# Token routing and the first expert blocks in one program, with the token numbers of two blocks computed on chip

## The reference

```python
h2 = rms_norm(x, norm_ffn_g)
y  = hierarchical_moe(h2, ...)
x  = x + y

def hierarchical_moe(h, ...):
    g_logits = h @ w_rg + b_rg                 # 4 groups
    grp      = argmax(g_logits)
    e_in     = (h @ w_re + b_re)[grp]          # 8 experts of that group
    top_p, top_e = top_k(softmax(e_in), 2)
    gate   = p_grp * top_p / sum(top_p)
    expert = grp * 8 + top_e                   # 2 of 32 experts for each token
    # assignments sorted by expert, each expert padded to blocks of 128 slots
    pos = pstart[expert] + rank_within_expert
    slot_tok[pos] = token
    for block:                                 # 128 slots, one expert
        gu = h[slot_tok] @ w_up[e];  g, u = split(gu)
        yb = (silu(g) * u) @ w_down[e]
    y[token] += gate * yb[pos]
```

## Time and profile before

| | |
|---|---|
| median of 3 runs | 1874.7 us (1873.71 to 1875.47) |
| profiled execution, its own time | 1877.97 us |
| its span | 1876.4 us |
| first instructions of `route` | 1201.1 us from the span's start |
| first transpose of `experts` on TensorE | 1265.2 us |
| transpose of block 2's tokens | 1291.9 us |
| busy share of the span | PE 91%, DVE 70%, ACT 44%, POOL 22% |

### The profile page before, as it was taken

The page is one execution under the profiler, slowest core; times in us unless marked ns, Lnnn a source line. Parts: engine busy times, 40 slices in busy tenths (PEclk is TensorE's granted clock), DMA queues, the critical chain, the costliest instruction groups (busy, mean ns, idle before and its releaser), DMA issues. The chain is left out here.

```text
span 1876.4 us, 25514 instructions
## 1 busy us (share of the span) xinstructions
PE 1704.8 (91%) x8546; PEld 1413.3 (75%) x8546; DVE 1322.0 (70%) x1800; ACT 823.3 (44%) x968; POOL 414.1 (22%) x311
## 2 busy tenths in 40 slices
PE   6999989999999988999969888509999999999995
PEld 5877778887888867899858677407888888887774
DVE  4257894899990028777449832446999999989895
ACT  5355321211121134567521211306777777767673
POOL 1211320232222210000012000052333232334342
PEclk8999999999999989999969899859999999999998
DMA  4722341332222546457076332429999999999992
GB/s 157 202 101 101 140 147 52 116 113 90 92 90 105 142 120 130 112 119 167 16 289 242 143 116 86 180 99 368 392 386 386 372 367 358 371 371 381 367 380 101
DMA packets 131388, 378.40 MB, mean 202 GB/s; under 512 B 37375, under 2 KB 41471, under 8 KB 131180
## 3 DMA queue, kind: packets, MB, share of 16 engines
q1 hardware_dynamic: 113764, 350.91, 53.7%
q0 software_dynamic: 17552, 26.54, 3.9%
HBM read 336.48 MB, written 67.63 MB: 215 GB/s over the span
## 5 line engine op out<-in xcount | busy, mean ns | idle before, releaser
L1664 DVE TENSOR_TENSOR ex_wl<-ex_raw,ex_wh 128x2048 fp32r<-128x2048 f32 x192 | 437.5, 2287 | 40.6 <-ACT ex_wh L1660 40.4
L1660 ACT ACTIVATE ex_wh<-ex_raw 128x2048 fp32r<-128x2048 f32 x192 | 367.8, 1919 | 143.6 <-PE ex_upp L2170 49.8
L76 PE MATMUL sg_gp<-hT_hi,gs_wh 128*128 128x512 f32 x512 | 200.5, 392 | 3.2 <-PEq L65 3.2
L77 PE MATMUL sg_gp<-hT_lo,gs_wh 128*128 128x512 f32 x512 | 199.8, 390 | 0.0
L78 PE MATMUL sg_gp<-hT_hi,gs_wl 128*128 128x512 f32 x512 | 199.8, 390 | 0.0
L796 ACT ACTIVATE gs_wh<-gs_raw 128x1024 fp32r<-128x1024 f32 x30 | 31.8, 1060 | 263.3 <-PE sg_gp L78 263.3
L1179 DVE TENSOR_TENSOR_SCAN at_keep<-at_t 128x128 f32<-128x128 f32 (+7 forms) x32 | 43.3, 1352 | 127.1 <-POOL at_keep L1107 122.5
L741 POOL TENSOR_TENSOR gs_wl<-gs_raw,gs_wh 128x1024 fp32r<-128x1024 f32 x30 | 72.1, 2403 | 251.1 <-ACT gs_wh L796 251.1
L1275 PE MATMUL at_ops<-at_v,at_pT 128*128 128x65 f32 (+1 forms) x984 | 125.1, 270 | 0.2 <-DVE at_o L1221 0.2
L1275 PEld LDWEIGHTS at_ops<-at_v,at_pT 128*128 128x128 f32 x984 | 120.5, 192 | 1.2 <-issue 0.4
L76 PEld LDWEIGHTS sg_gp<-hT_hi,gs_wh 128*128 128x128 f32 x512 | 96.4, 188 | 24.3 <-issue 4.2
(11 more groups left out here) (286 smaller groups left out, 3885.9 us busy)
## 6 DMA issues: line engine op xcount, KB each, us to landing
ex_raw<-in_w_expert_up SPq DMA_DIRECT2D x128, 1024.0 KB, 21.1
ex_raw<-in_w_expert_down SPq DMA_DIRECT2D x64, 1024.0 KB
gs_raw<-in_w_gate SPq DMA_DIRECT2D x32, 512.0 KB
gatesT<-sg_go SPq DMA_DIRECT2D x32, 512.0 KB, 2.6
mg_g<-gatesT SPq DMA_DIRECT2D x8, 2048.0 KB
...
```

Source lines behind the costliest of these rows:

```text
L76: pe.matmul(out, a_hi, b_hi, start=(k == 0), stop=False)
L77: pe.matmul(out, a_hi, b_lo, start=False, stop=False)
L1660: act.activation(ring.wh[r][:, :, :], ring.raw[slot][:, :, :], ACT.Copy).then_inc(ring.w_high, 1)
L1664: dve.tensor_tensor(ring.wl[r][:, :, :], ring.raw[slot][:, :, :], ring.wh[r][:, :, :].bitcast(F32), ALU.subtract).then_inc(ring.w_low, 1)
```

## The change

`route` and `experts` become one program, `route_and_experts`, without a barrier between them. In it:

- DVE's chain is shorter. One product and one sum over groups take the place of seven steps for `ein`. One product for each choice writes `full` as bf16 for all 32 experts. Each choice has its own place in `full`, and `both` is gone.
- TensorE sums the counts: two products with ones give the counts in each tile, 16 more add the counts of all earlier tiles to the ranks, so the eight `prefix` additions are gone. Both choices' positions come from one product and one sum.
- The token numbers of blocks 0 and 1 are found without `slots`: DVE compares the positions with 0 to 127 (`find`, two comparisons of 128x1024 for a block), TensorE multiplies the one-hot by token numbers (16 products of 2 columns), and POOL gathers from that, ahead of the 16 scatters. `slots` is read from block 2 on.
- `eblk` is made with one expert block in each partition (32 columns instead of 1600) and turned to a row by one product.
- The gates are computed at the end of the chain, after the first two blocks' numbers.
- POOL clears `xg`, and makes the low part of the first weight piece (128x2048). The other three of block 0 are made by DVE: one before block 0's tokens, two between block 0's and block 1's.
- SP waits for `planned` before it loads block 1's weights. Before, the barrier stood there.

```diff
-        route(nc, a, lg, eblk, pairs, slots, ring)
-        experts(nc, a, ident, eblk, pairs, slots, h2d, out, ring)
+        route_and_experts(nc, a, ident, lg, eblk, pairs, slots, h2d, out, ring)
...
+        ids_ps = c.enter_context(nc.psum_tensor("rt_ids", [P, 2, 2], F32))
...
+        prod = xa[1][:, 0:2 * NT * EXPERTS].rearrange("p (k t e) -> p k t e", k=2, t=NT)
+        by_group = xa[1][:, 512:768].rearrange("p (t q j) -> p t q j", t=NT, q=GROUPS)
+        slot = xa[1][:, 768:1024].rearrange("p (t e) -> p t e", t=NT)
+        at_spot = [t[:, :].bitcast(BF16).rearrange("p (t s) -> p t s", t=NT) for t in (gl, act_)]
+        cmp = xa[0][:, 0:EXPERTS * NT].rearrange("p (e t) -> p e t", e=EXPERTS)
+        ranks = yp[:, 0:NT * EXPERTS].rearrange("p (t e) -> p t e", t=NT)
+        sums = yp[:, HALF:HALF + NT * EXPERTS].rearrange("p (t e) -> p t e", t=NT)
+        row = ap_[0:1, 0, :]
+        consts = sem("rt_consts")
...
+            for j in IN_ROUTE:
+                load_pair(sp, a, ring, j, 0, j - FIRST)
+            for j in range(UP_PAIRS, PAIRS):
+                load_pair(sp, a, ring, PAIRS + j, 0, j)
+            sp.wait_ge(planned, 1)
             n = trips(sp)
             expert = lambda b: sp.value_load(eblk[0:1, bass.ds(b, 1)], min_val=0, max_val=EXPERTS - 1)
...
+            def first_max(oh, scores, top, rank, work, k):
+                step(dve.tensor_tensor(work, scores, bc(top, [P, NT, k]), ALU.is_equal))
+                step(dve.tensor_tensor(work, work, rank.unsqueeze(1).to_broadcast([P, NT, k]), ALU.mult))
+                step(dve.tensor_reduce(peak[:, :, :], work, AX, ALU.max))
+                step(dve.tensor_tensor(oh, work, bc(peak[:, :, :], [P, NT, k]), ALU.is_equal))
+            def spread(k):
+                step(dve.tensor_tensor(full[:, k, :, :].rearrange("p t (j q) -> p t j q", q=GROUPS),
+                                       eoh[k][:, :, :].unsqueeze(3).to_broadcast([P, NT, PER_GROUP, GROUPS]),
+                                       goh[:, :, :].unsqueeze(2).to_broadcast([P, NT, PER_GROUP, GROUPS]), ALU.mult))
+            dve.wait_ge(consts, 2)
+            step(dve.tensor_reduce(m0[:, :, :], g, AX, ALU.max))
+            step(dve.tensor_tensor(gs[:, :, :], g, bc(m0[:, :, :], G4), ALU.subtract))
+            marks["group"] = done[0]
+            first_max(goh[:, :, :], g, m0[:, :, :], rank4[:, :], esc[:, :, 0:GROUPS], GROUPS)
+            step(dve.tensor_tensor(by_group, e, goh[:, :, :].unsqueeze(3).to_broadcast(QJ), ALU.mult))
+            step(dve.tensor_reduce(ein[:, :, :].unsqueeze(3), by_group.rearrange("p t q j -> p t j q"), AX, ALU.add))
+            step(dve.tensor_reduce(m1[:, :, :], ein[:, :, :], AX, ALU.max))
+            first_max(eoh[0][:, :, :], ein[:, :, :], m1[:, :, :], rank8[:, :], esc[:, :, :], PER_GROUP)
+            step(dve.scalar_tensor_tensor(ein[:, :, :], eoh[0][:, :, :], PICKED, ein[:, :, :], ALU.mult, ALU.add))
+            step(dve.tensor_reduce(m2[:, :, :], ein[:, :, :], AX, ALU.max))
+            first_max(eoh[1][:, :, :], ein[:, :, :], m2[:, :, :], rank8[:, :], esc[:, :, :], PER_GROUP)
+            for k in range(2):
+                spread(k)
+            marks["full"] = done[0]
+            step(dve.tensor_tensor(ratio[:, :, :], m2[:, :, :], m1[:, :, :], ALU.subtract))
+            marks["ratio"] = done[0]
+            dve.wait_ge(consts, CONSTS)
+            dve.wait_ge(summed_up, 1)
+            S = [P, EXPERTS, NT]
+            step(dve.tensor_reduce(count[:, :].unsqueeze(2), sums.rearrange("p t e -> p e t"), AX, ALU.add))
+            step(dve.tensor_tensor(cmp, count[:, :].unsqueeze(2).to_broadcast(S),
+                                   steps[:, :].unsqueeze(1).to_broadcast(S), ALU.is_gt))
+            step(dve.tensor_reduce(nblk[:, :].unsqueeze(2), cmp, AX, ALU.add))
+            step(dve.tensor_tensor_scan(bend[:, :], nblk[:, :], nblk[:, :], 0.0, ALU.add, ALU.max))
+            step(dve.tensor_tensor(base[:, :], bend[:, :], nblk[:, :], ALU.subtract))
+            dve.wait_ge(ranked, 1)
+            step(dve.scalar_tensor_tensor(slot, base[:, :].unsqueeze(1).to_broadcast([P, NT, EXPERTS]), float(P), ranks,
+                                          ALU.mult, ALU.add))
+            step(dve.tensor_tensor(prod, full[:, :, :, :], slot.unsqueeze(1).to_broadcast([P, 2, NT, EXPERTS]), ALU.mult))
+            step(dve.tensor_reduce(posf[:, :, :].unsqueeze(3), prod, AX, ALU.add))
+            def find(b, positions):
+                for k in range(2):
+                    step(dve.tensor_tensor(at_spot[k], spot[:, :].unsqueeze(1).to_broadcast([P, NT, P]),
+                                           positions[:, k, :].unsqueeze(2).to_broadcast([P, NT, P]), ALU.is_equal))
+                    marks["at_spot", b, k] = done[0]
+            def number_tokens(b):
+                dve.wait_ge(ids_summed, b + 1)
+                dve.tensor_scalar(ids_x[b][:, 0:1], ids_ps[:, b, 0:1], ids_ps[:, b, 1:2], float(T), ALU.add,
+                                  ALU.add).then_inc(ids_ready, 1)
+            find(0, posf)
+            step(dve.tensor_scalar(posf1[:, :, :], posf[:, :, :], -float(P), None, ALU.add))
+            step(dve.scalar_tensor_tensor(bcmp[:, :], bend[:, :], bcol[:, 0:1], stride[:, :], ALU.is_le, ALU.mult))
+            step(dve.tensor_reduce(ebcol[:, :], bcmp[:, :], AX, ALU.add))
+            marks["ebcol"] = done[0]
+            number_tokens(0)
+            step(dve.tensor_tensor(halfc[:, :], bend[0:1, EXPERTS - 1:EXPERTS].to_broadcast([1, MAX_BLOCKS // 2]),
+                                   evens[:, :], ALU.is_gt))
+            step(dve.tensor_reduce(half[:, :], halfc[:, :], AX, ALU.add))
+            step(dve.tensor_scalar(pairs[:, :], half[:, :], -1.0, None, ALU.add))
+            dve.wait_ge(row_made, 1)
+            dve.tensor_copy(eblk[:, :], row[:, 0:MAX_BLOCKS + 2]).then_inc(planned, 1)
+            dve.wait_ge(ids_ready, 1)
+            find(1, posf1)
+            step(dve.tensor_copy(pos[:, :, :], posf[:, :, :]))
+            dve.wait_ge(e_done, 2)
+            step(dve.tensor_reduce(gsum[:, :, :], gsc[:, :, :], AX, ALU.add))
+            step(dve.reciprocal(pg[:, :, :], gsum[:, :, :]))
+            step(dve.tensor_scalar(rsum[:, :, :], rinv[:, :, :], 1.0, None, ALU.add))
+            step(dve.reciprocal(rsum[:, :, :], rsum[:, :, :]))
+            number_tokens(1)
+            step(dve.tensor_tensor(gate[0], pg[:, :, :], rsum[:, :, :], ALU.mult))
+            step(dve.tensor_tensor(gate[1], gate[0], rinv[:, :, :], ALU.mult))
+            marks["entry"] = done[0]
+            def low_in_route(p):
+                dve.wait_ge(ring.w_low, p)
+                dve.wait_ge(ring.w_high, p + 1)
+                split_low(dve, ring, p, p % RING)
...
+            low_in_route(IN_ROUTE[1])
             x_lo(0, 0)
+            for p in IN_ROUTE[2:]:
+                low_in_route(p)
             x_lo(1, 1)
+            for tile in xa:
+                dve.memset(tile[:, :], 0.0).then_inc(cleared, 1)
             low(0, 0, 0)
             gate_up(0, position(0, 0))
             low(0, 0, 1)
             low(0, 0, 2)
+            dve.wait_ge(planned, 1)
+            n = trips(dve)
...
+            const(pool.iota(number[:, :, 0], pattern=[[0, NT]], base=-P, channel_multiplier=1, **F))
+            const(pool.iota(number[:, :, 1], pattern=[[P, NT]], base=P - T, channel_multiplier=0, **F))
+            const(pool.iota(spot[:, :], pattern=[[1, P]], base=0, channel_multiplier=0, **F))
+            const(pool.iota(bcol[:, :], pattern=[[0, 1]], base=0, channel_multiplier=1, **F))
...
+            pool.dma_start(slots.rearrange("(p n) a -> p n a", p=P), empty[:, :, :]).then_inc(emptied, 16)
+            pool.sem_inc(ring.w_loaded[0], 16)
+            pool.sem_inc(ring.w_loaded[1], 16)
+            for tile in xg:
+                pool.memset(tile[:, :], 0.0).then_inc(cleared, 1)
+            pool.memset(ids_o[1][:, :], T).then_inc(nobody, 1)
+            p = IN_ROUTE[0]
+            pool.wait_ge(ring.w_high, p + 1)
+            pool.tensor_tensor(ring.wl[p % RING][:, :, :], ring.raw[p][:, :, :], ring.wh[p % RING][:, :, :].bitcast(F32),
...
+            for s in range(2):
+                pool.wait_ge(cleared, 2)
+                pool.wait_ge(ids_ready, s + 1)
+                pool.indirect_dma_start(xg[s][:, :], None, h2d[:, :],
+                                        bass.IndirectOffsetOnAxis(ap=ids_x[s][:, 0:1], axis=0), **rows).then_inc(gathered[s], 16)
+            pool.wait_ge(consts, CONSTS)
+            pool.wait_ge(emptied, 16)
+            pool.wait_ge(d, marks["entry"])
+            for q in range(2):
+                for t in range(NT):
+                    pool.indirect_dma_start(slots[:, :], bass.IndirectOffsetOnAxis(ap=pos[:, q, t:t + 1], axis=0),
+                                            entry[:, q, t, :], None).then_inc(placed, 16)
+            pool.wait_ge(placed, 16 * 2 * NT)
+            for s in range(2):
```

(45 more changed lines are left out.)

453 lines of the change are left out of this document (164 added, 289 removed).

## The result

The changed kernel takes 1862.62 us (median of 4, 1861.54 to 1863.44), the one before 1874.45 in the same comparison (4 runs): ratio 0.9929, 95% interval 0.9917 to 0.9942 (the two medians alone give 0.9937, inside that interval). Faster, by 11.8 us where I forecast 19.2. The profiled execution took 1863.44 us with a span of 1861.8; against the profiled one of before that is 14.5 less, since that one lay 3.5 over this median and this one 0.8 over its own.

The account below looks back on a forecast made before the run. TensorE was taken to set the pace first, DMA from between 1500 and 1600 us. Block 2's transposes 23.2 us earlier, less 4.0 for the clock, save 19.2: 1874.7 to 1855.5 us, range 1845 to 1869.

Parts of the forecast that it names:

- the clock: TensorE falls to half clock during its idle time before block 2; warming up again costs 4.0 us, bounds 0 and 5.1.
- the new wait: TensorE finishes blocks 0 and 1 at 1255.7, then stands idle 13 us until block 2's tokens come.
- The chain to the positions: DVE's steps from the router's end to the tokens' positions, with TensorE's counts and ranks: positions there at 1216.6.
- the lock: POOL's low-part subtraction holds DVE's 512-wide product with two SBUF inputs for 3.7 us, bounds 0 and 4.7.
- Token numbers: Comparisons and products behind the positions: block 0's numbers at 1220.4, block 1's at 1225.1, first scatter at 1226.6.
- Scatters: POOL's 16 scatters take 25.5 us as before, to 1252.1; bounds 20.3 and 39 us.
- Landing: From the last scatter until ids can be asked for, weights loading beside it: 4.0 us, between 2.2 and 6.7.
- Ids: Loading block 2's token ids from the table takes 4.66 us from issue, as before; could take 6.7.
- A: Rival: shorter path, with no lock, scatters at lower bound and fast landing, 11 us more saved, 1844.6; chance 0.13.
- B: Rival: nearly all scatters run under DVE's subtractions and need 39 us, 13.5 us more, 1869; chance 0.13.
- C: Rival: scatters drain slowly behind queued weights, 4.5 us per 128 pieces, landing at 1298.6, 42.5 us more, 1898; chance 0.05.
- D: Rival: block 0's tokens land after 1242, so its 26.7 us of work end after 1268.7; chance 0.02.

Follow-up runs that it names:

- experiment 6: Changed kernel with the tiles for a third block's token numbers declared but unused, no instruction differing: 1857.81 us, ratio 0.9909.
- experiment 9: Kernel before the change, with an unused tile of 128 bytes a partition ahead of the expert tiles: 1874.48 us against 1876.16, ratio 0.9993.
- experiment 1: Changed kernel with the first weight piece's low part made by VectorE behind its chain instead of by POOL: 1856.71 us, ratio 0.9906.
- experiment 7: Changed kernel with block 2's tokens also found on chip, and the first weight piece's low part on VectorE instead of POOL: 1852.02 us, ratio 0.9878.
- experiment 8: Experiment 7's kernel with block 0's output rows fetched early, behind the sixteenth scatter, with ids found on chip: 1849.71 us, ratio 0.9866.
- experiment 2: Changed kernel with the second choice's eight scatters issued once more to an unread spare table, ids waiting for all 24: 1869.08 us, ratio 0.9960.
- experiment 5: Changed kernel measured again, unchanged, beside later runs: 1861.01 us, ratio 0.9924.
- experiment 10: Changed kernel with an unused tile of 224 bytes a partition ahead of the expert tiles: 1858.01 us, ratio 0.9904.
- experiment 4: Changed kernel with block 2's tokens found on chip too, its gather issued between the fourth and fifth scatter: 1856.04 us, ratio 0.9896.

## Why the prediction was right, and where it was off

**The sum.** Against 19.2 us forecast the two traces show 14.6. The way to block 2 gave 5.8 less than forecast, and the clock cost 1.8 less. Four effects had no term: the router's end lay 1.1 later, the part behind the last transposes took 1.4 longer, the slower steady period lost 2.0, and the last blocks came 3.9 cheaper. That these come to only 0.6 us lost is luck. The 2.7 between the profiled executions' 14.5 and the medians' 11.8 come from which executions were profiled. The mechanism was right: the new wait, its place and its releaser.

**What bounds the kernel.** "An earlier start of TensorE's steady work moves the whole rest of the stage with it, provided the ring is full when it starts" holds: 528.7 and 528.9 us from there to the last transposes. But the ring's head start is a stock that the loop eats up. In the last blocks DMA sets the pace; between 1700 and 1800 us ACT, which splits first, waits for the raw pieces of the changed kernel (us in total, times, longest):

```profile
ACT ex_wh L1659 <- DMA ex_raw<-in_w_expert_up: 26.6, 22, 2.1
```

There a block takes 18.9 to 19.0 us, while TensorE needs 18.05 to 18.12. The changed kernel's 26 blocks at 18.12 use 26 x 0.8 = 21 us of the stock; before used 23 x 0.9 = 20; the moved ones (experiments 6 and 9) used 20 x 1.2 = 24 and 18 x 1.2 = 22. By this working the ring's 12 pieces are worth some 20 to 24 us, and the changed kernel ends just as they run out. I had seen the waits of SP fade, and did not draw from them that a faster TensorE is soon worth nothing, as experiment 9 shows. The ring was full only about when TensorE resumed, not by 1265 as forecast: the DMA share is 1.02 until 1272 and 0.70 in the next 4 us. That DMA "costs nothing" was right and gave something back: in the 16 us in which TensorE stood the ring filled up. Experiments 6 and 9, which share the period of 17.71, give its size: from block 3's transposes to the last ones 505.5 us against 508.3, so 2.8 us. The rest of the 3.9 in the table is the other side of the slower period, at which the stock lasts longer.

**The chain to the positions.** Forecast 16.5 us behind the router's end, measured 16.8. The parts differ: the lock was 4.8 us and not 3.7, the wait for the ranks not there at all (the last 14 products took 1.7 us, beside the lock). That DVE would stand until POOL is done was right, and the Trainium skill's rule (SBUF — State Buffer, "SBUF: two separate sides") agrees with 5.20 us for a step of 0.42 and with its return in experiment 1. That the one which starts first keeps the port, as the same section has it, the rows don't show: DVE's began 0.38 us ahead of POOL's and was the one held. The step named was wrong: ACT split the first piece at 1207.49, 1.7 us earlier than the earlier trace rows shows for before, so POOL began when its clearing was done, 1.3 us earlier from the router's end than forecast, and met the comparison of the counts instead of the 512-wide product.

**Token numbers.** Block 0's at 20.3 us behind the router's end, forecast 20.3; `entry` at 25.1, forecast 25.4. The first scatter was forecast at 26.5 and came at 28.6. The step "two gathers, each about 1 us" failed: 1.80 and 2.62, the second under DVE's first subtraction. I had the row for it: a scatter takes 1.9 to 2.3 under a subtraction, and a gather is issued the same way.

**Scatters.** 26.8 against 25.5. **Landing** 5.55 against 4.0: inside 2.2 to 6.7, and I took a middle where the weights' traffic was as in the loop. **Ids** 5.9 against 4.66, for which I named 6.7 as possible. **Gather** 7.6 against 7.9. In sum block 2's transposes came 74.4 us behind the router's end where 68.6 was forecast: 2.0 from the gathers, 1.3, 1.5 and 1.3 from scatters, landing and ids, less 0.3. These four mis-sized terms make up most of the miss. Landing and ids say the same: a small transfer beside full weight traffic costs nearly what it costs in the loop, not what it cost when the queues were empty. Gathers and scatters say another thing: an issue on POOL under a subtraction of DVE takes 1.9 to 3.6 us instead of 1.

**The clock.** Forecast 4.0, measured 2.2; the half clock was granted, for 4 us and not for the 10 us that followed the first start of before.

**The place of the tiles.** No step of mine had it. New tiles moved the stationary operands by 5408 bytes, and a block went from 18.05 to 18.12 us: 2.0 us in this trace. At the old remainder the changed kernel has 0.9904 and not 0.9929 or 0.9924, which would be 18 us; how much of that is the place, the intervals don't settle.

**Rivals.** A (shorter path): no, though experiments 1, 7 and 8 are versions of it. B (scatters under DVE): 26.8 us, no; with DVE busier, 32.0 in experiment 1. C (drain): excluded by experiment 2, where 24 scatters land 5.03 us behind the last. How many descriptors a packet of this kernel holds, no run showed, so the Trainium skill's rule on turns between queues (DMA: Bandwidth & Descriptors, "Queues, rings and completion order") is neither shown nor refuted; a landing of 5.0 to 6.7 us behind the last scatter, in place of the 2.2 of the earlier trace rows, is all that is seen. D: no, block 0 started at 1230.32, forecast "near 1229".

**Signs named beforehand.** None of the three for being wrong came: the scatters' issue took 26.8 us and their landing 5.6, TensorE stood idle ahead of block 2, and SP's waits between 1300 and 1400 are still 71.3 us. Those for being right: first transpose near 1229: 1230.32. About 13 us idle, a DMA as releaser: 16.25. Clock 0.5 behind it: yes. The 512-wide product 4 us: no, 0.69. 16 scatters in 25 us: 26.8. Paces of the loop as before: almost, and the small difference led to experiments 5, 6, 9 and 10.

What stays open: why the remainder of an address matters to TensorE, and whether the high parts, the low parts or both carry it, since all moved together, and the expert program's other tiles with them. Why POOL's chain in experiments 4, 7 and 8 takes seven blocks to catch up isn't settled either: the fetch alone it isn't, and no run took block 3's ids out of the slots.
